# A transformer and mixture-of-experts kernel: the first expert pair's tokens fetched from memory, expert loads reordered, a shorter router product

## What is computed

```python
h2 = _modulate(_rms(x, norm2_g[l]), sh2, sc2)          # rms(x) * g * (1 + sc2) + sh2
logits = einsum('btd,de->bte', h2, w_r)
aff = softmax(logits)                                  # over 16 experts
gate, idx = top_k(swapaxes(aff, 1, 2), 64)             # 64 tokens for each expert
xe = h2[idx]                                           # [16, 64, 1024]
ye = einsum(silu(xe @ w_g) * (xe @ w_u), w_d) * gate
x = x + g2 * scatter_add(ye, idx)
```

## Time and profile before

| | |
|---|---|
| runs | 1280.94, 1281.85, 1278.98 us; median 1280.94 |
| the profiled execution | 1281.94 us, its span 1279.8 us |
| PE busy | 1264.9 us, 99% of the span |
| DVE, ACT, POOL busy | 747.0 (58%), 509.8 (40%), 509.1 us (40%) |
| chain that ended last | PE 90%, DVE 6%, DMA 1%, ACT 1% |
| HBM read, written | 221.86 MB, 4.19 MB |

### The profile page before, as it was taken

One profiled execution on the slowest core, in us unless ns is written; L12 is line 12 of the kernel. 1 busy time (PEld: TensorE's weight loads), 2 busy tenths in 40 slices (PEclk: granted clock), 3 DMA queues, 4 the chain that ended last, 5 costly groups with the idle time before them and its releaser, 6 DMA issues.

```text
span 1279.8 us, 16632 instructions
## 1 busy us (share of the span) xinstructions
PE 1264.9 (99%) x6452; PEld 944.8 (74%) x6452; DVE 747.0 (58%) x1333; ACT 509.8 (40%) x765; POOL 509.1 (40%) x284
## 2 busy tenths in 40 slices
PE   8999999999999999999999999999999999999998
PEld 6789888766687544443466788888889889889887
DVE  2487986877854434322358558322686586576453
ACT  4353324476433211111256742333454354344343
POOL 3154457277430000000052252544458458548630
PEclk9999999999998899999999999999999999999999
DMA  9534585101157899999942121322113323313301
GB/s 384 227 133 180 204 332 187 33 34 66 67 218 284 316 426 426 426 426 426 427 188 99 67 99 66 132 99 99 50 62 125 111 66 124 130 47 121 125 1 66
DMA packets 34350, 227.13 MB, mean 177 GB/s; under 512 B 3936, under 2 KB 4576, under 8 KB 9440
## 3 DMA queue, kind: packets, MB, share of 16 engines
q1 hardware_dynamic: 31536, 216.63, 43.8%
q10 hardware_dynamic: 1584, 5.24, 1.1%
q0 software_dynamic: 1152, 4.19, 0.9%
HBM read 221.86 MB, written 4.19 MB: 177 GB/s over the span
## 4 chain that ended last, share of the span: by engine, by line
PE 90%; DVE 6%; DMA 1%; ACT 1%; issue 1%; SPq 0%; DVEq 0%; ACTq 0%
PE psum L1150 22%; PE psum L1152 22%; PE psum L1151 22%; PE psum L1706 13%; PE psum L1476 2%; DMA mod_in<-in_stream 1%; PE psum L1441 1%; DVE x L2879 1%; PE psum L1791 1%; DVE psum L3189 1%; PE psum L1691 1%; PE psum L1666 1%; PE psum L1694 1%; PE psum L1649 0%; DVE acc_g L3199 0%
## 5 line engine op out<-in xcount | busy, mean ns | idle before, releaser
L1116 POOL TENSOR_TENSOR log_lo<-raw,log_hi 128x1024 fp32r<-128x1024 f32 (+1 forms) x102 | 181.7, 1804 | 131.1 <-ACT log_hi L2004 130.8
L1065 POOL TENSOR_TENSOR w_lo<-raw,w_hi 128x1024 fp32r<-128x1024 f32 x43 | 106.2, 2469 | 312.1 <-ACT w_hi L2025 307.0
L1150 PE MATMUL psum<-b_hi,log_hi 128*128 128x512 f32 x384 | 149.6, 390 | 0.0
L1151 PE MATMUL psum<-b_lo,log_hi 128*128 128x512 f32 x384 | 149.4, 389 | 0.0
L1152 PE MATMUL psum<-b_hi,log_lo 128*128 128x512 f32 x384 | 149.4, 389 | 0.0
L1069 POOL TENSOR_TENSOR w_lo<-raw,w_hi 128x1024 fp32r<-128x1024 f32 x43 | 112.0, 2606 | 0.0
L2025 ACT ACTIVATE w_hi<-raw 128x2048 fp32r<-128x2048 f32 (+1 forms) x44 | 83.2, 1892 | 46.3 <-PE psum L1152 23.5
L1706 PE MATMUL psum<-ex_ring,xe 128*64 128x512 f32 x432 | 95.0, 594 | 0.0
L1150 PE MATMUL psum<-b_hi,w_hi 128*128 128x512 f32 x224 | 88.5, 395 | 0.1
L1152 PE MATMUL psum<-b_hi,w_lo 128*128 128x512 f32 x224 | 87.3, 390 | 0.0
L1151 PE MATMUL psum<-b_lo,w_hi 128*128 128x512 f32 x224 | 87.2, 389 | 0.0
(11 more groups left out here) (507 smaller groups left out, 2968.7 us busy)
## 6 DMA issues: line engine op xcount, KB each, us to landing
raw<-in_stream SPq DMA_DIRECT2D x88, 1024.0 KB, 5.0
ex_ring<-in_stream SPq DMA_DIRECT2D x78, 1024.0 KB, 16.8
ex_more<-in_stream SPq DMA_DIRECT2D x18, 1024.0 KB, 18.0
raw<-in_stream SPq DMA_DIRECT2D x12, 768.0 KB, 4.3
mod_in<-in_stream SPq DMA_DIRECT2D x8, 1024.0 KB, 20.8
x<-in_x SPq DMA_DIRECT2D x4, 512.0 KB, 5.5
x<-in_x ACTq DMA_DIRECT2D x1, 2048.0 KB, 7.8
xt<-h2t ACTq DMA_DIRECT2D x8, 256.0 KB, 8.7
```

The costliest lines, as they stand in the source:

```text
L1065: nc.gpsimd.tensor_tensor(w_lo[:, slot, w], raw[:, raw_slot, w], w_hi[:, slot, w].bitcast(F32), ALU.subtract)
L1116: nc.gpsimd.tensor_tensor(lo_, src, hi_.bitcast(F32), ALU.subtract).then_inc(w_lo_done, 1)
L1150: mm(o, w[0], x[0], start=start, stop=False, skip_group_check=goes_on)
L1151: mm(o, w[0], x[1], start=False, stop=False, skip_group_check=goes_on)
```

## The change

Six things:

1. Both halves of pair 0's tokens are fetched: `picked` is gone, `fetched(0)` to `fetched(3)` stand ahead of chunk 0, behind the indices of pairs 0 and 1 and the transposed slots.
2. Chunks 5, 6 and 7 are loaded only after the eight token tiles have landed (`EX_HELD`, a wait for `xt_in`).
3. Chunk 0 has a buffer of its own (`ex_first`), loaded with chunks 9 and 8; its slot takes chunk 17, in chunk 0's old place of `EX_FIRST`. The first load that waits for `ex_used` is chunk 18.
4. DVE multiplies shift and router and sums over the eight blocks (two operations of 128 elements a partition, long before), so that PE does one product with ones in place of eight.
5. `ranks` takes three products of double width in place of six.
6. `rounded_products`, of ones in fp32r (one record each), fill waits: four ahead of `aff_t`, two in place of one `idle_products` ahead of `ranks`, eight ahead of the fetched tokens.

The core of the diff:

```diff
-EX_FIRST = [11, 12, 13, 14, 15, 16, 0, 1, 2, 3, 4, 5, 6, 7]
-EX_EARLY, EX_LATE = (9, 8), 10
+EX_FIRST = [11, 12, 13, 14, 15, 16, NEX, 1, 2, 3, 4, 5, 6, 7]
+EX_EARLY, EX_LATE = (9, 8, 0), 10
+EX_HELD = 5
...
+        ex_first = at("ex_first", R + 72, [P, CH])
+
         def ex(m):
+            if m == 0:
+                return ex_first[:]
             s = EX_SLOT[m % NEX]
...
+                if m == EX_HELD:
+                    sp.wait_ge(xt_in, 16 * len(X_TOK))
                 load_ex(m)
...
-            for m in range(NEX, PAIRS * EX_CHUNKS):
+            for m in range(NEX + 1, PAIRS * EX_CHUNKS):
...
+            def rounded_products(n, bank):
+
+                for _ in range(n):
+                    mm(psum[:, bank, :], ones_r[:], ones_r[:, 0:1].to_broadcast([P, T]), start=True, stop=True)
...
-            shift = open_tile("shift_r")
-            shift_rows(0)
             done(logit_rows(1))
             last_columns(0, sq, 2)
             rcols[0] += 1
-            done(shift_rows(1))
+            o = open_tile("shift_r")
+            pe.wait_ge(shift_summed, 1)
+            done(mm(o[:, 0:NE], ones[:], shift_s[:], start=True, stop=True))
...
             for t, half in X_TOK[:2]:
                 x_tok(t, half)
+            pe.wait_ge(tri_done, 1)
+            rounded_products(4, 0)
             o = open_tile("aff_t")
...
-            idle_products(1, 0)
+            rounded_products(2, 0)
...
-            for s in range(2):
-                for t in range(1, TT):
-                    mm(ranks[:, s, t:TT, :], ones_r[:], marks[:, s, t - 1:t, :].to_broadcast([P, TT - t, NE]),
-                       start=False, stop=False)
+            for t in range(1, TT):
+                mm(ranks[:, :, t:TT, :], ones_r[:], marks[:, :, t - 1:t, :].to_broadcast([P, 2, TT - t, NE]),
+                   start=False, stop=False)
...
             wide_products(1, 0)
             token_ids(0)
-            picked(0)
             token_ids(1)
...
-            picked(1)
+            rounded_products(8, 0)
+            for c in range(4):
+                fetched(c)
...
                     if i == 0 and c == 1:
-                        fetched(2)
-                        fetched(3)
                         token_ids(2)
                         places(0)
...
+            link(V.tensor_tensor(shift_p[:], router[:], mod[:, 3 * KD:4 * KD, 0].unsqueeze(2).to_broadcast([P, KD, NE]), ALU.mult))
+            V.tensor_reduce(shift_s[:], shift_p[:].rearrange("p k e -> p e k"), AX.X, ALU.add).then_inc(shift_summed, 1)
```

More of the change, by code:

```diff
@@ L478, in make_plan @@
     p.add("ids", 0, by=("ids_done", 1), bank=5)
-    p.add("xq", 0, by="act", bank=7)
     p.add("ids", 1, by=("ids_done", 2), bank=6)
     p.add("slots_t", bank=2)
+    p.add("xq", 0, by="act", bank=7)
     p.add("xq", 1, by="act", bank=5)
@@ L734, in build @@
         lg_sb = at("lg_sb", R + 90, [P, T])
+        shift_p = at("shift_p", R + 89, [P, KD, NE])
+        shift_s = at("shift_s", R + 89.5, [P, NE])
         xg = at("xg", R + 32, [P, 2, D])
@@ L745, in build @@
         work = at("work", R + 114, [3 * NE, 2 * P])
[L746 to L749, removed]
+        lists = at("lists", R + 115, [3 * NE, CAP])
+        list_b = at("list_b", R + 115.25, [NE, CAP])
+        top_m = at("top_m", R + 115.5, [NE, CAP])
+        limit = at("limit", R + 115.75, [NE, 1])
         slots_r = at("slots_r", R + 120, [P, T], F32R)
@@ L805, in build @@
         ex_full = [sem(f"ex_full{i}") for i in range(NEX)]
+        ex_first_full = sem("ex_first_full")
         ex_used = sem("ex_used")
@@ L860, in build @@
         router_g_done = sem("router_g_done")
+        shift_summed = sem("shift_summed")
         rcol_done = sem("rcol_done")
@@ L992, in load_ex @@
             def load_ex(m):
-                sp.dma_start(ex(m), stream[len(CHUNKS) + m, :, :]).then_inc(ex_full[m % NEX], 16)
+                sp.dma_start(ex(m), stream[len(CHUNKS) + m, :, :])\
+                    .then_inc(ex_full[m % NEX] if m else ex_first_full, 16)
             for i, m in enumerate(EX_FIRST):
@@ L1571, in logit_rows @@
                 return last
[L1573 to L1579, removed]
             def x_tok(t, half):
@@ L1617, in _ @@
             pe.wait_ge(freed_act, PLAN.freed_count(TILE["x_tok", TT - 1, 1]))
-            idle_products(1, 0)
+            rounded_products(2, 0)
             o = open_tile("ranks")
-            pe.wait_ge(tri_done, 1)
             pe.wait_ge(freed_dve, PLAN.freed_count(TILE["work_t"]))
@@ L1640, in token_ids @@
                     last = mm(o[:, 0:n], pick_tok[:, i % 4, t, :], tok_affs[:, t, i, 0:n], start=t == 0, stop=t == TT - 1)
[L1641 to L1650, removed]
                 done(last)
@@ L1696, in expert_chunk @@
             def expert_chunk(m):
-                pe.wait_ge(ex_full[m % NEX], 16 * (m // NEX + 1))
+                if m == 0:
+                    pe.wait_ge(ex_first_full, 16)
+                else:
+                    pe.wait_ge(ex_full[m % NEX], 16 * (m // NEX + (m % NEX != 0)))
                 return ex(m)
```

## The result

| | before | change |
|---|---|---|
| median of 14 runs each | 1280.47 us (1278.98 to 1281.85) | 1283.18 us (1282.70 to 1284.19) |
| ratio | | 1.0023, interval 1.0016 to 1.0030 |
| span of the profiled execution | 1279.8 us | 1281.5 us |
| PE busy | 1264.9 us | 1259.2 us |

The change makes the kernel slower, by 2.7 us or 0.2%, which the interval tells from nothing. The forecast was 1279.5 us, a gain.

What follows compares the result with a forecast made beforehand. PE, busy for 99% of the span, was taken as the bound; chunk 2 coming 1.4 us earlier gave 1281.94 - 1.4 = 1280.5 us for the profiled execution, 1279.5 us against the median of 1280.94, range 1276.9 to 1282.1.

Steps and rivals of the forecast that it cites:

- To the logits: Without the shift products on PE, L1569 starts 0.7 us earlier and the logits' products (L1601) end 2.5 us earlier.
- What the rounded products give back: Ahead of the affinities, rounded products at half clock leave 1.1 us of the 2.5 us gained; affinities at about 406.1.
- rival A: Clock stays up or falls late: affinities 2.5 us earlier, fetch lands about 423.1, gain 3.3 us, 1277.6 us; chance 0.30.
- DVE's two operations: The added shift operations ahead of the low parts, 0.6 us together, covered by 1.2 us and costed at nothing.
- Stores and loads: Token tiles in memory at about 414, chunk 7 landed at 424.1, the fetch of pair 0 landed at 425.0.
- bound of 8.6 us: Longest time for the fetch of pair 0, beside deep queues of loads: landing at 427.5; alone it takes 4.5 us.
- To chunk 2: From the fetch's landing through transposes and chunks 0 and 1 to chunk 2: 6.3 us; gain 1.4 us.
- chunk 2 starts 6.3 us behind the landing: PE's stretch behind the fetch: 1.3 us of transposes, copies and hand-overs, 3.6 for chunks 0 and 1, 1.4 to chunk 2.
- the gain is 426.4 less the landing time: At chunk 2, a fetch landing before 426.4 gains the difference; with a landing at 425.0, 1.4 us.
- B: The fetch of pair 0 becomes the bound, landing at 427.5 beside held loads: 1.1 us loss, 1282.0 us; chance 0.14.
- hard form: Late store or half-clock rounded products also shift loads and fetch by 1.5 us: loss 2.6 us, 1283.5 us; chance 0.07.
- C: Expert loads are the bound: an earlier PE runs into chunk 95 after 2.6 us, capping the gain at 1278.3; chance 0.03.

Runs made afterwards that it cites:

- picked kernel: The change with the first half of pair 0 picked by products again, without the eight rounded products, against the kernel before: 1278.04 us against 1279.97, ratio 0.9987.
- filled change: The change with 30 rounded products instead of 8 ahead of the fetched tokens, against the kernel before: 1283.03 us against 1279.97, ratio 1.0022.

## Why the prediction was wrong

**To the logits**: right in its order and sizes. L1569's successor started at 399.42 for 398.85 predicted, 0.56 of the difference being the later M, and the four-product group was gone.

**What the rounded products give back**: wrong in both profiles of the change. I took the fall at 401.6 for given. The clock stayed up, the products took 1.1 us, PE waited 0.52 us for the affinities, and these came 2.8 us earlier counted from M: rival A's first half.

**DVE's two operations**: 0.29 and 0.37 us, 0.66 in all for 0.6 predicted, and no wait of PE came of them.

**Stores and loads**: the times came out, in part by luck. The stores were in memory at 414.0 for 414 predicted, the fetch landed at 425.4 for 425.0, although it left 0.8 us earlier. But the forecast had the affinities 8.5 us behind M (406.1), and they came at 6.8; the last store went out at 410.2, 1.3 before the 411.5 forecast. It then took 3.8 us, where I had taken 2.6 from a store with nothing beside it, and the errors cancelled. Under rival A, whose early affinities came true, I had put the landing at 423.1. What was right is the mechanism: the fetch landed 0.4 us behind the last of the three loads. The bound of 8.6 us was met nearly, with 8.5, in the run with 24 products.

**To chunk 2**: here the prediction failed, twice.
First, "chunk 2 starts 6.3 us behind the landing" was 8.9 (9.0 in the second profile). With the clock up it is 6.6, by three profiles; the other 2.3 us go with records at half clock (3.61 us for chunk 0 against 1.94, 1.94 for the transposes against 1.03). I had worked out that PE would wait, even named the eight products as lying inside that wait, and costed the idle time at nothing. In both profiles of the change the transposes and chunk 0 then ran at half clock, which they did in none of the three of before. That the idle time causes it isn't shown by these two alone: in the second the clock fell at 416.6, ahead of the wait. The runs with 30 products, of which five had no fall, speak for it; their time says that this step alone doesn't carry the loss.
Second, "the gain is 426.4 less the landing time" was measured against one draw of before, in which the picks had run at half clock. Counted from M, the point of no gain is 28.8 us there, but 25.7 and 26.9 in the other two profiles of before (chunk 2 behind M, less 6.3). The landing came at 27.3 and 27.5. So even the 6.3 would have meant a loss of 0.4 to 1.8 us against those. The removed term, two groups of picks for 3.76 us and more, is 2.0 us each with the clock up, and what the change saves by it goes into the wait for the fetch that it creates. I had seen that the profiled execution lay 1.0 us above the median, and carried its difference over whole.

**The rivals.** B's mechanism came true: the fetch became the bound and the loads stood beside it (taking them away gave back 2.7 us). Its price was wrong: it put the loss at landings behind 426.4, and 425.4 already loses. That its hard form says 1283.5, near the 1283.2 measured, is luck, as it wanted a landing 1.5 us behind 427.5. A's early affinities came true and led only to a longer wait. C did not come, and the extra chunk ahead was rightly costed at nothing: in the change PE waits for no weights from 396 to 660. The sum of the loss by the rows, from the second profile of before: 4.2 us, of which 1.9 are the landing with 6.6 behind it and 2.3 the clock. From the mean of the three (33.5) it is 2.7 to 3.0 us, of which the landing is about 0.5. This split is of single executions; the five runs without a fall don't bear out that the 2.3 us can be had back by themselves.

What stays open: how much of the 1.6 us of holding in the picked kernel is the fetch, and where the time goes in the executions of the filled change in which the clock doesn't fall; none of the profiles here shows such a one.

The best version found keeps everything of the change but the fetched first half and the eight products ahead of it: 1278.04 us.

## What to carry to other kernels

Work that PE does in place of waiting for a transfer costs only what it takes beyond that transfer: before removing it, work out when the transfer lands, and compare with when the work ends in several executions, not one. A stage whose clock falls at a different place in each execution wants several profiles and the clock of every run before a loss is put down to it: here filling the gap kept the clock up in five of 11 executions and didn't give the time back. Products that end behind the transfer are a delay of their own. And a fetch that the first product waits for should have no large loads issued between its data's stores and itself.

## What was unexpected

- The clock's falls move between executions of one program: 401.6 and 418.7, 402.8, or 402.0 in three profiles of the same kernel, for 6.8 or 10.2 us. The Trainium skill, "TensorE: Matmul & The Clock Gate", section "What's actually happening", says that this moment isn't tied to the kernel's start; the trace agrees, with the places just given. The stretch to chunk 2 differs by 3.2 us between these profiles (32.0 to 35.2).
- Products meant to keep the clock up don't always do so: eight, seventeen or 24 of them ran at half clock in the draws in which it had fallen just ahead of them.
- The fetch of pair 0, 0.5 MB, took 4.2 to 4.6 us with no expert loads beside it and 6.1 to 8.5 us with the three held loads beside it, though they come from another queue.
